# Walking the last slabs of two output projections tile by tile, with the next norm woven in

## The reference, cut to what matters

```python
# first block
mixed = jnp.concatenate([o_gdn, o_mla], axis=-1) @ w_out[l]
x = x + rms_norm(mixed, mix_post_norm[l])
h = rms_norm(x, ffn_pre_norm[l])
f = jnp.square(jax.nn.relu(h @ w_up[l])) @ w_down[l]
...
# second block
mix_out = merged @ w_out[l]
x = x + gt1[:, None, :] * rms_norm_2(mix_out, g_post_mix[l])
h2 = modulate(rms_norm_2(x, g_pre_mlp[l]), sh2, sc2)
ff = jnp.square(jax.nn.relu(h2 @ w_mlp_in[l])) @ w_mlp_out[l]
```

## Time and profile before

| what | value |
|---|---|
| median of 3 runs | 3057.18 us (3056.59 to 3060.26) |
| profiled execution | 3053.83 us |
| its span on the chip | 3051.8 us |
| PE busy | 2887.0 us, 95% of the span |
| POOL busy | 1047.9 us, 34% |
| DVE busy | 1586.0 us, 52% |
| ACT busy | 739.1 us, 24% |

### The profile page before, as it was taken

The page is one execution under the profiler, slowest core; times in us unless marked ns, Lnnn a source line. Parts: engine busy times, 40 slices in busy tenths (PEclk is TensorE's granted clock), DMA queues, the critical chain, the costliest instruction groups (busy, mean ns, idle before and its releaser), DMA issues.

```text
span 3051.8 us, 42710 instructions
## 1 busy us (share of the span) xinstructions
PE 2887.0 (95%) x16394; PEld 2324.2 (76%) x16394; DVE 1586.0 (52%) x1925; ACT 739.1 (24%) x1486; POOL 1047.9 (34%) x738
## 2 busy tenths in 40 slices
PE   7998898979899999999899999989998999999998
PEld 6886567868788888888678886657876888888886
DVE  3464544662777777777832004773234455445545
ACT  3323564323311111111420004552124101110111
POOL 4321001348534333333543321212358232323232
PEclk9999999999999999999999999999999999999999
DMA  3210000013222222222221111001132111111111
GB/s 123 56 27 11 11 4 23 3 49 128 74 90 76 82 82 82 84 82 89 88 65 43 54 31 32 22 1 56 62 118 62 49 46 50 50 46 45 51 50 61
DMA packets 213436, 172.15 MB, mean 56 GB/s; under 512 B 15543, under 2 KB 188878, under 8 KB 213326
## 3 DMA queue, kind: packets, MB, share of 16 engines
q1 hardware_dynamic: 160670, 135.47, 14.1%
q10 hardware_dynamic: 52656, 35.13, 3.8%
HBM read 162.19 MB, written 8.39 MB: 56 GB/s over the span
## 4 chain that ended last, share of the span: by engine, by line
PE 83%; DVE 6%; POOL 4%; ACT 3%; issue 2%; DMA 1%; SPq 0%; POOLq 0%; DVEq 0%; ACTq 0%
PE ps L921 13%; PE ps L923 12%; PE ps L922 12%; PE ps L1338 8%; PE ps L1339 7%; PE ps L1340 7%; PE ps L1130 2%; PE ps L1048 2%; PE ps L940 1%; PE ps L942 1%; PE ps L941 1%; POOL rstd L721 1%; PE ps L1070 1%; PE ps L1276 1%; PE ps L1521 1%
## 5 line engine op out<-in xcount | busy, mean ns | idle before, releaser
L292 POOL TENSOR_SCALAR slab_hi<-raw 128x1024 fp32r<-128x1024 f32 (+1 forms) x236 | 266.2, 1128 | 1523.4 <-PE ps L923 567.3
L295 POOL TENSOR_TENSOR slab_lo<-raw,slab_hi 128x1024 fp32r<-128x1024 f32 (+1 forms) x236 | 577.8, 2448 | 19.7
L921 PE MATMUL ps<-act_hi,slab_hi 128*128 128x512 f32 x1472 | 577.0, 392 | 5.8 <-DVE act_lo L2086 4.0
L923 PE MATMUL ps<-act_hi,slab_lo 128*128 128x512 f32 x1472 | 574.8, 391 | 0.0
L922 PE MATMUL ps<-act_lo,slab_hi 128*128 128x512 f32 x1472 | 574.5, 390 | 0.0
L2484 DVE TENSOR_TENSOR acc<-ps,acc 128x512 f32<-128x512 f32 x512 | 339.7, 686 | 212.9 <-PE ps L1340 212.7
L1338 PE MATMUL ps<-slab_hi,hid_hi 128*128 128x512 f32 x1024 | 405.0, 395 | 11.3 <-DVE hid_lo L2475 8.9
L1339 PE MATMUL ps<-slab_hi,hid_lo 128*128 128x512 f32 x1024 | 401.1, 392 | 0.0
L1340 PE MATMUL ps<-slab_lo,hid_hi 128*128 128x512 f32 x1024 | 400.4, 391 | 0.0
L1889 ACT ACTIVATE relu<-ps 128x512 f32<-128x512 f32 x128 | 77.0, 602 | 1037.5 <-PE ps L923 1013.8
L921 PEld LDWEIGHTS ps<-act_hi,slab_hi 128*128 128x128 f32 x1472 | 277.5, 189 | 64.1 <-issue 3.3
(11 more groups left out here) (319 smaller groups left out, 4200.9 us busy)
## 6 DMA issues: line engine op xcount, KB each, us to landing
raw<-in_w_in SPq DMA_DIRECT2D x56, 512.0 KB, 3.7
w_ada<-in_w_ada ACTq DMA_DIRECT2D x48, 512.0 KB, 4.0
raw<-in_w_out SPq DMA_DIRECT2D x32, 512.0 KB, 3.5
raw<-in_w_up SPq DMA_DIRECT2D x32, 512.0 KB, 4.0
raw<-in_w_down SPq DMA_DIRECT2D x32, 512.0 KB, 3.5
raw<-in_w_mlp_in SPq DMA_DIRECT2D x32, 512.0 KB, 4.0
raw<-in_w_mlp_out SPq DMA_DIRECT2D x32, 512.0 KB, 3.5
x_tok<-in_x SPq DMA_DIRECT2D x8, 512.0 KB, 6.2
```

What stands on the lines that cost most here:

```text
L292: pool.tensor_scalar(self.hi[s][:, 0:width], self.raw[r][:, 0:width], 1.0, 0.0, ALU.mult, ALU.add)\
L295: pool.tensor_tensor(self.lo[s][:, 0:width], self.raw[r][:, 0:width], self.hi[s][:, 0:width].bitcast(F32), ALU.subtract).then_inc(self.spl ...
L921: pe.matmul(o, hi[:, w], a_hi[:, k, cols], start=(k == 0), stop=False)
L923: mm = pe.matmul(o, lo[:, w], a_hi[:, k, cols], start=False, stop=(k == nk - 1))
```

## The change

On PE, slabs 0 to 12 are walked as before, slab by slab. Slabs 13, 14 and 15 are then walked tile by tile: all three for tile 4, then for tile 5, 6, 7. The wait for slab 15 comes ahead of the first of these, and the three slabs are given back with tile 7. The two halves of the first turn follow tiles 4 and 6 instead of slabs 13 and 14. `up(0)` waits for each k of the first split instead of for all of it. On ACT, DVE and POOL the norms of the late tiles are interleaved with the first turn, and on POOL the splits of slabs 17 and 18 move behind norms of late tiles.

```diff
@@ -519,9 +519,10 @@
+        LATE_NORMS = ((0, 4), (0, 5), (1, 4), (0, 6), (1, 5), (0, 7), (1, 6), (1, 7))
         NORM_ORDER = [("n1", t) for t in range(NT)]
         for halves in (("mix_post", "n2"), None, ("mix_post2", "n4")):
-            NORM_ORDER += [(tag, t) for part in (EARLY, LATE) for tag in halves for t in part] if halves else FFN_NORMS
+            NORM_ORDER += [(tag, t) for tag in halves for t in EARLY] + [(halves[n], t) for n, t in LATE_NORMS] if halves else FFN_NORMS
@@ -830,12 +831,15 @@
                 ffn_splits(following, 0, range(1))
-                for j in range(2):
-                    if pre in SHIFTED:
-                        norm_hi(pre, 0, range(4 * j, 4 * j + 4))
-                    ffn_splits(following, 0, range(1 + j, 2 + j))
-                norm_rstd(post, LATE)
-                norm_rstd(pre, LATE)
+                for n, t in LATE_NORMS:
+                    if (n, t) == (0, NT - 1):
+                        ffn_splits(following, 0, range(1, 2))
+                    norm_rstd((post, pre)[n], [t])
+                    if pre in SHIFTED and (n, t) == (0, 4):
+                        norm_hi(pre, 0, range(4))
+                    if pre in SHIFTED and (n, t) == (0, 6):
+                        norm_hi(pre, 0, range(4, KD))
+                ffn_splits(following, 0, range(2, 3))
                 if pre in SHIFTED:
                     norm_hi(pre, 1)
@@ -1295,7 +1299,7 @@
-                for m in range(16):
+                for m in range(13):
@@ -1307,9 +1311,18 @@
-                    if m in (13, 14):
+                ring.ready(pe, 0, 15)
+                for t in range(4):
+                    for m in range(13, 16):
+                        mm = out_tile(ring, m, t, a_hi, a_lo)
+                        if t == 3:
+                            mm.then_inc(ring.used, 1)
+                        elif m == 15:
+                            mm.then_inc(sem("mixed_prod"), 1)
+                    if t == 0:
                         pe.wait_ge(sem("mixed_done"), 16 * run + 12)
-                        turn(pre, acc, 0, scaled(pre, 0), ks=range(4 * (m - 13), 4 * (m - 13) + 4))
+                    if t in (0, 2):
+                        turn(pre, acc, 0, scaled(pre, 0), ks=range(2 * t, 2 * t + 4))
@@ -1378,9 +1391,7 @@
-                    if first:
-                        turn_done(pre, 0)
-                    up(i, 0)
+                    up(i, 0, as_split(pre, 0) if first else None)
@@ -1858,12 +1869,29 @@
-                norm_full(pre, 0, act_hi, scale, bias)
-                for t in range(4):
+
+                def late(t):
                     take(1, 1, t)
                     act.wait_ge(sem("mixed_done"), 16 * run + 12 + t + 1)
                     norm_square(post, 4 + t, acc, junk)
-                pre_norm(pre, 2 * run, LATE)
+
+                def late_square(t):
+                    act.wait_ge(sem("resid_done"), NT * 2 * run + t + 1)
+                    norm_square(pre, t, resid, junk)
+
+                late(0)
+                norm_full(pre, 0, act_hi, scale, bias, ks=range(4))
+                late(1)
+                late_square(4)
+                late(2)
+                norm_scale(pre, 4)
+                norm_full(pre, 0, act_hi, scale, bias, ks=range(4, KD))
+                late_square(5)
+                late(3)
+                norm_scale(pre, 5)
+                for t in (6, 7):
+                    late_square(t)
+                    norm_scale(pre, t)
                 norm_full(pre, 1, act_hi, scale, bias)
@@ -2440,9 +2468,17 @@
-            for h, tiles in enumerate((EARLY, LATE)):
-                post_norm("mix_post", mix_post_row, tiles, lambda t: dve.wait_ge(sem(f"x_in{t}"), 32))
-                norm_split("n2", h, act_hi, act_lo, ffn_pre_gain)
+            def post_norms(post, pre, row, ready, gain=None):
+
+                post_norm(post, row, EARLY, ready)
+                post_norm(post, row, (4,), ready)
+                norm_split(pre, 0, act_hi, act_lo, gain, ks=range(4))
+                post_norm(post, row, (5,), ready)
+                norm_split(pre, 0, act_hi, act_lo, gain, ks=range(4, KD))
+                post_norm(post, row, (6, 7), ready)
+                norm_split(pre, 1, act_hi, act_lo, gain)
+
+            post_norms("mix_post", "n2", mix_post_row, lambda t: dve.wait_ge(sem(f"x_in{t}"), 32), ffn_pre_gain)
@@ -2656,9 +2692,7 @@
-            for h, tiles in enumerate((EARLY, LATE)):
-                post_norm("mix_post2", gate_rows[0], tiles, lambda t: dve.wait_ge(sem(f"x_in{t}"), 48))
-                norm_split("n4", h, act_hi, act_lo)
+            post_norms("mix_post2", "n4", gate_rows[0], lambda t: dve.wait_ge(sem(f"x_in{t}"), 48))
```

## The result

| kernel | median | runs | profiled execution | its span |
|---|---|---|---|---|
| before | 3058.91 us (3056.59 to 3060.61) | 8 | 3053.83 us | 3051.8 us |
| changed | 3066.31 us (3061.83 to 3069.81) | 8 | 3062.90 us | 3060.9 us |

The ratio is 1.0025, 95% interval 1.0015 to 1.0035: 7.6 us slower (the medians themselves differ by 7.4). The forecast was 3065.3 us, +8.1.

The account below looks back on a forecast made before the run. PE carries 83% of the chain; run 0 moves with T, run 1 with POOL's memset. 5.5 + 2.1 + 0.5 = +8.1 us gives 3061.9 profiled, 3065.3 median; own range 3063.3 to 3069, wider range 3058.5 to 3069.5.

Parts of the forecast that it names:

- The wait for slab 15: PE stands before slab 13 until POOL has split slab 15: 4.9 us in run 0, 5.1 in run 1.
- The clock: After that stand PE's granted clock falls to 0.5, costing 2.0 us per run, with ends 1.4 and 3.1.
- T: Start of PE's second turn; forecast at 789.3 in run 0, 5.5 us lost, and at 2339.1 in run 1.
- a stand before `up(1)`: PE waits for slab 17, whose split on POOL stands behind late norms: 2.0 us in run 0, 2.9 in run 1.
- the rival in which the roots slip past: POOL's small root operations do not wait for DVE's port; sum +5.8 us, or +4.6; chance 0.33 including a cheap clock.
- its strict form: The port as exclusive lock for whole instructions; shrinks run 1's difference between orders by 1.2 us, sum +6.9.
- From T to `down` in run 0: Stays 23.62 us, plus 0.5 for a slab load sharing DMA engines with `w_ada`; bounds nothing or 1.3 us.
- Run 1's memset: POOL's memset, which run 1's `down` waits for, ends at 2360.2 against 2358.1 laid out before; loses 2.1 us.
- The slabs-in-time case: Slab 15 split by 748.2, no stand or lost clock; run 0's T 1.6 us earlier, 3055.2 us; chance 0.04.
- The remark that the interleaving alone is worth 2 us: Drawn from the layout without stand or lost clock: interleaving gains only 2 us, since slabs 17 and 18 hold up roots.

Follow-up runs that it names:

- e5: The changed kernel once more, without an edit, for the scatter; ratio to before 1.0025.
- e1: The changed kernel with PE waiting for each of slabs 13, 14 and 15 where first used, not for 15 ahead of all; ratio to before 0.9988.
- e6: The changed kernel with a wait for each of slabs 13 to 15 at first use, plus eight unread products before tile 4's slab 15; ratio to before 0.9986.
- e3: The changed kernel with slab 17 split on POOL right behind tile 6's first root, before tile 7's; ratio to before 1.0027.
- e4: The kernel before with PE's new tile-by-tile walk alone, norms in their old order; one run, 3081.71 us to 3056.66.
- e2: The changed kernel with twenty unread products keeping PE busy while it waits for slab 15; ratio to before 1.0023.
- e7: Only slabs 14 and 15 walked tile by tile, each waited for when needed, slab 17 split before the late roots; ratio to before 0.9989.
- e8: The changed kernel's order of norms on the old slab-by-slab walk, splits at their old places; one run, 3062.20 us to 3057.29.
- e12: The changed kernel with twenty unread products during the wait for slab 15, run a second time unedited; ratio to before 1.0026.
- e9: Slabs 14 and 15 alone walked tile by tile, with the first two w_ada transfers issued ahead of the norms; ratio to before 0.9975.

## Why the prediction was right, point by point

**The wait for slab 15** was sized 4.9 and 5.1 us and measured 4.65 and 4.93, then 4.66 and 5.00 in e5. e1 and e6 show that it is the main cause. That the whole came out at +8.0 for +8.1 is in part luck: the same kernel once more, e5, gives +9.1.

**The clock**, 2.0 per run: three `out_tile`s lie between the restart and the first half of the turn, 4.09 us at full clock. They took 763.54 - 757.79 = 5.75 and 2315.73 - 2309.15 = 6.58, so 1.7 and 2.5 were lost. The six other such restarts on record (e3, e4, e5) took 5.82 to 6.88 us, so 1.7 to 2.8 were lost, 2.4 in the mean of all eight: within the bounds of 1.4 and 3.1, a little above 2.0. What e2 does not settle is whether this price is paid in most executions.

**T.** From the first product of slab 13 the layout had 36.2 us (run 0) and 37.3 (run 1); the trace has 35.59 and 37.41. Inside, the forecast of a stand before `up(1)` holds, 1.33 and 2.33 us against 2.0 and 2.9. POOL's timeline of the changed kernel shows its two reasons:

```profile
779.96 1.15 POOL L719 TENSOR_SCALAR mean_sq<-ssq 128x1 f32<-128x1 f32 x1 [3.58 <-ACT squares_junk L1597]
781.20 1.54 POOL L722 TENSOR_TENSOR rstd<-mean_sq,minus_half 128x1 f32<-128x1 f32 x1
782.71 1.05 POOL L292 TENSOR_SCALAR slab_hi<-raw 128x1024 fp32r<-128x1024 f32 x1
783.85 2.37 POOL L295 TENSOR_TENSOR slab_lo<-raw,slab_hi 128x1024 fp32r<-128x1024 f32 x1
786.30 0.19 POOL L719 TENSOR_SCALAR mean_sq<-ssq 128x1 f32<-128x1 f32 x1
```

The root of tile 5 met DVE's operation of 779.78 and 781.10 and was held by it, 1.54 us instead of 0.55, as the earlier trace rows had it for the old order. So the rival in which the roots slip past did not come. In this the Trainium skill ("SBUF — State Buffer", section "SBUF: two separate sides") agrees with the trace again; its strict form would have given run 1 a loss of 0.9 us (2.1 less 1.2), measured was 1.7, between the two. Tile 7 had been squared at 781.5, and its root began at 786.30, behind the split.

**From T to `down` in run 0** the forecast kept 23.62 us and added 0.5. Measured: 24.53, so 0.9. Here a term was mis-sized. Queues of SP and ACT in the changed kernel, and DVE for the arrivals:

```profile
795.77 3.86 SPq L283 DMA_DIRECT2D raw<-in_w_up  x2
```
```profile
798.60 2.49 ACTq L1903 DMA_DIRECT2D w_ada<-in_w_ada  x2
```
```profile
803.36 1.23 DVE L2488 TENSOR_TENSOR w_ada<-w_ada,vec_cols 128x1024 f32<-128x1024 f32 x1 [3.24 <-DMA w_ada<-in_w_ada]
...
806.66 1.23 DVE L2488 TENSOR_TENSOR w_ada<-w_ada,vec_cols 128x1024 f32<-128x1024 f32 x1 [0.56 <-DMA w_ada<-in_w_ada]
```

The forecast counted one slab load beside `w_ada`. There are two, since the splits of slabs 18 and 19 now follow one another at 792.0 to 799.0, and each frees a buffer. The first `w_ada` took 803.36 - 798.60 = 4.76 us until DVE used it, where before it took 792.91 - 788.88 = 4.03, and DVE stood 0.56 for the second. That second one sets the loss: DVE takes it up 806.66 - 793.38 = 13.28 us after T, before 795.56 - 783.19 = 12.37, and from there to `down` both kernels need 11.25. The 0.9 lies within the bounds of nothing and 1.3 us.

**Run 1's memset** was laid out to end 58.4 us after slab 13's first product; `down` began 2367.88 - 2309.15 = 58.7 after it. The change's loss there is 1.7, forecast 2.1.

**The slabs-in-time case** was priced at -1.6 for T of run 0. No run makes that case: in e6 tile 4 still waits for slab 15, only that eight products fill the wait of some 1.8 us. Its T of run 0 is 1.3 us later than before, its stretches are 0.8 us shorter in all. e7 with its own order reaches -1.9. The remark that the interleaving alone is worth 2 us can hold with the new walk only: without it, e8 shows a loss of 5.8.

**Still open:** why e2 and e12 do not run faster than the changed kernel although their profiled stretches are 4 us shorter, and why e1 runs 3.7 us faster than before although its profiled stretches are 2.1 longer. The mean granted clock of every execution is on record and narrows this. Averages over the executions of a kernel, each difference with a standard error of about 0.0005:

| kernel | granted clock | before, same chip |
|---|---|---|
| e5 changed again | 0.9775 | 0.9781 |
| e2 kept busy | 0.9777 | 0.9782 |
| e12 the same again | 0.9784 | 0.9789 |
| e1 ready each | 0.9799 | 0.9782 |
| e6 each and busy | 0.9796 | 0.9781 |

Within a kernel the executions with a clock lower by 0.001 are 1.8 us longer; if PE were busy throughout it would be 3.1 us (an estimate: 0.001 of 3057). So e1's executions lose, by this estimate, 3 to 5 us less to the clock than those of before, which is about the size of the 3.7. The profiled executions do not show it: their clocks are 0.979 (e1) and 0.980 (before). Where in the execution e1 gains this clock no run shows. In e2 and e12, 4 us saved would raise the clock by 0.0013 over the changed kernel's; both lie 0.0005 below before, the changed kernel 0.0006. So what the added products saved in the two profiled stretches does not show in the average execution as a whole. Whether the clock falls behind the stand in the others all the same, or falls elsewhere, no experiment tells apart.

## What to carry to other kernels

A reordering that finishes tiles sooner needs all of its operands at the start of the walk, not at its end: look up when the last operand is ready before choosing how many slabs to interchange, and interchange one fewer if it isn't. Wait at the first use of each operand. Count also what each moved operation gives back (a slab pair, a raw buffer, a load), since that sets who collides next.

## What was not expected of the hardware

- The granted clock fell to 0.50, the lower of its two levels, behind two stands of only 0.87 and 1.79 us, with 8.6 us of work between them (e1, run 0). It was at 1.00 again by 760, 5 us after the restart. With stands of 0.84 and 0.21 us it stayed at 1.00 (e2).
- The same code takes other times from one execution to the next: the start of slab 12 in run 0 varied over 6.8 us among the profiled executions, though no edit of the study lies ahead of it. The clock has a part in it: in the first 100 us it was 1.00 in the trace of before and 0.97 in that of the changed kernel, which reach slab 12 at 742.61 and 747.40.
- DVE operations on two SBUF inputs took 2.77 us instead of 0.69 beside POOL's split (e9, and `hid_lo` 2.72 in the kernel before).
